# A tenth SBUF home for expert tiles, TensorE's experts written out, down bias behind the transposes, last tile in three pieces, output stores from two queues

## The chip, the cores and the metric

One core of one Trainium2 chip. The metric is the device time of one execution of the program, in microseconds (us).

## The reference

One inference step of a one-layer trunk, over T = 320 tokens (256 of a prompt, 64 of a sample) with 1024 features, in float32:

```python
x += W_out [ GatedDeltaNet heads | MLA heads ]( RMSNorm(x) )
x += MemXAttn( RMSNorm(x), mem )          # 4 heads, 256 memory tokens
x += MoE( RMSNorm(x) )                    # top 4 of 32 experts, softmax router

# MoE, for each expert e and its tokens xb
gu = xb @ w_gu[e] + b_gu[e]               # 1024 -> 2048
gt = min(gu[:, :1024], 7); up = clip(gu[:, 1024:], -7, 7)
act = gt * sigmoid(1.702 * gt) * (up + 1)
y = act @ w_down[e] + b_down[e]           # 1024 -> 1024, then times the gate, summed per token
```

The weights of one expert are 8 MB (w_gu) and 4 MB (w_down); all 32 experts are read.

## The kernel before, in words

**Before the experts** (up to about 360 us) come the input projection, the delta-rule heads, the latent attention, the output projection (its matmuls count the semaphore x2_mm), the attention over the memory and the router. SyncE (SP) issues all weight loads from one queue, each behind `wait_ge` on the semaphores that say that the place in SBUF is free.

**The expert stream.** An expert's weights are TILES = 6 tiles of 2 MB: four of w_gu (GT = 4, each 256 rows of K) and two of w_down (512 rows each). Tile number n (0 to 191) goes to home n % SLOTN of SLOTN = 9 homes of 16 KB a partition (`slot_sb`, L277, `tile_at`, L279): six lie in the tensor `weights`, one each in `stream`, `small_weights` and `more_weights`. Nine tiles are loaded before the experts start (`first_tiles`, L544 to L558), each as soon as its place is free: tiles 2 to 5, then 8, 0, 7, 6, and 1. From then on tile n is issued when TensorE has used tile n - 9 (`refill`, L560: `wait_ge(tile_used)`, then one DMA, in a loop of 18 tiles, which are 3 experts). One DMA is spread over 16 DMA engines, and its semaphore is full when all of them have landed their part.

**One expert on TensorE** (`expert`, L1920): `gate_up` (L1844) multiplies the gathered tokens, 64 of them, with four tiles and lays the scatter of the expert before between them (matmuls with the one-hot rows `slotT`, then DVE's `accumulate`, L2576, adds into x); `gather` (L1832) collects the tokens of the next expert with 60 bf16 matmuls, and `slots_to_rows` makes three transposes; `down` (L1878) waits for the activation, transposes it (four transposes, L1125), waits for ScalarE's copies of them (`copies`, L1099) and multiplies with the two w_down tiles; ScalarE then copies the 64 rows out. The bias of w_down is put into the PSUM bank first by `down_bias` (L1838, two bf16 matmuls, with the row selector `sel` that DVE's `select`, L2482, writes), called in `gate_up` behind the second k. Experts 1 to 30 stand in a hardware loop of ten turns with three experts each (L1926); expert 31 is written behind it (L1929), expert 0 ahead of it. Where the program says `matmul` on float32 the trace shows two weight loads and two matmuls.

**On DVE** a loop over experts (accumulate, `slotT` copy, one-hot slots, activations, `select`, and `rows_in`, L2555, which copies the gathered tokens out) runs beside it. What follows the last expert is a branch for experts with more than 64 tokens, which these inputs do not take (no instruction of it is in the trace).

**The end.** The last scatter gives five halves of x. DVE adds each (L2584), and SP stores it once `acc_done` says so (`store_half`, L576 to L580): six DMAs from SP's queue, the fifth and the sixth both behind the fifth addition.

**Tables.** The router's small tables (`KT`) lie in `stream`, `om` (the memory attention's output) and `wr_sb` (the router's weights) in the first part of it.

Of the kernel before, what the change touches and what calls it, by code (L numbers as in the profile page):

```python
# [15 lines left out]
BF16 = mybir.dt.bfloat16  # L16
# [5 lines left out]
P = 128  # L22
# [66 lines left out]
def trunk_kernel(nc, x_prompt, x_sample, cache_kv_latent, cache_k_rope, state_gdn, state_conv, cache_mem_k,  # L89
# [5 lines left out]
    with ctx:  # L95
# [162 lines left out]
        om = V[:, 4352:5632].rearrange("p (h t) -> p h t", h=H)  # L258
# [17 lines left out]
        GT, TILES, SLOTN, TURN = 4, 6, 9, 3  # L276
        slot_sb = [W[:, 4 * FF * n:4 * FF * (n + 1)] for n in range(6)] + [VK[:, 5888:9984], RH[:, 2816:6912], W2[:, :]]  # L277
# [4 lines left out]

        def fixed(e):

            return [tile_at(TILES * e + t) for t in range(TILES)]

        def turned(i, c):

            return [(ap, name, i * (16 * TURN * TILES // SLOTN) + count)
                    for ap, name, count in (tile_at(TILES * (1 + c) + t) for t in range(TILES))]  # L290

        def extra(j):

            return [(slot_sb[t], f"ld_slot{t}", j * 16 + 16 * ((TILES * E - t + SLOTN - 1) // SLOTN + 1)) for t in range(TILES)]
# [10 lines left out]
        wr_sb = V[:, 5632:5888].rearrange("p (k n) -> p k n", k=KD)  # L305
# [10 lines left out]
        rpos = KT[:, 256:388].rearrange("p (b e) -> p b e", b=TB + 1)  # L316
        xg_pair = PS[4][:, :].rearrange("p (a k t) -> p a k t", a=2, k=4)
        lg = KT[:, 452:560].rearrange("p (b e) -> p b e", b=TB)
        mrep = KT[:, 560:668].rearrange("p (b e) -> p b e", b=TB)
        top8 = KT[:, 668:692].rearrange("p (b e) -> p b e", b=TB)  # L320
        rep8 = KT[:, 692:716].rearrange("p (b e) -> p b e", b=TB)
        S = KT[:, 716:908].bitcast(BF16).rearrange("p (b a s) -> p b a s", b=TB, a=2)
        identb, ustrictb, onesb = (X[:, 2560 + 64 * i:2624 + 64 * i].bitcast(BF16) for i in range(3))
        id3 = X[0:96, 2752:2769].bitcast(BF16)
        cnt, tot, start = KT[0:E, 988:989], KT[0:E, 989:990], KT[0:E, 990:991]
        flags, pos4 = KT[0:E, 992:996], KT[0:E, 996:1000]
        hot = KT[0:E, 1000:1128].rearrange("p (b s) -> p b s", b=XTRA)
        xlist = KT[:, 1128:1200].bitcast(I32)
        ntop = KT[:, 1200:1203]
        gsum = KT[:, 1203:1206]  # L330
# [31 lines left out]
        for b in range(2):  # L362
            for h in range(H):
# [4 lines left out]
                                  [[vm_p[:, i, h * P:(h + 1) * P] for i in range(2)]], om[:, h:h + 1, qs]))  # L368
        qs, ks = slice(2 * P, T), slice(SEQ, NKEY)
        for h in range(0, H, 2):  # L370
# [6 lines left out]
                              [[vm_s[:, i, j * P:(j + 1) * P] for i in range(2)] for j in two], om[:, h:h + 2, qs]))  # L377
# [54 lines left out]


# [4 lines left out]
        def _(sp):  # L438
# [137 lines left out]
            def store_half(b, half):  # L576
                cols = slice(512 * half, 512 * half + 512)
                dst = yp[0][b * P:(b + 1) * P, cols] if b < 2 else ys[0][:, cols]
# [6 lines left out]
            with sp.If(n_extra > 0):  # L585
# [6 lines left out]
                for n in range(2 * TB):  # L592
                    store_half(n // 2, n % 2)
# [2075 lines left out]
```

## Time and profile before

| | us |
|---|---|
| median of 3 runs | 1284.6 (1284.45 to 1285.82) |
| the profiled execution's own time | 1286.58 |
| its span (first to last instruction) | 1284.8 |
| TensorE busy in the span | 1252.6 |
| DVE busy | 436.9 |
| ScalarE busy | 207.1 |

The profiled execution took 1.78 us more than its span, and 1.98 us more than the median. "PE" is TensorE's matmuls, "PEld" its weight loads, "SPq" what SyncE's queue issues, L and a number a line of the kernel. L1122 and L1125 are helpers through which all matmuls and all plain transposes go.

### The profile page before, as it was taken

What the parts mean: (1) busy time and instruction counts of PE and PEld (TensorE: products, weight loads), DVE (VectorE), ACT (ScalarE), POOL (GpSimd) and SP (SyncE); (2) the same over time, 40 slices, a digit from 0 to 9 for tenths busy, and PEclk for the clock granted to TensorE, in tenths of its full rate; (3) what the DMA queues carried; (4) which work ended last, traced back from release to release, by engine and by line L of the source; (5) the groups of instructions that cost most, each with busy time, mean ns of one, the idle gap of its engine ahead of it and who ended that gap; (6) DMA issues with size and microseconds to landing.
All of it is one profiled execution on the core that took longest, in us unless ns stands there. A gap on an engine that the chain in (4) does not pass through costs nothing.

```text
span 1284.8 us, 20003 instructions
## 1 busy us (share of the span) xinstructions
PE 1252.6 (97%) x8107; PEld 569.6 (44%) x8107; DVE 436.9 (34%) x970; ACT 207.1 (16%) x551; POOL 17.2 (1%) x30
## 2 busy tenths in 40 slices
PE   8999999999999999999999999999999999999997
PEld 6677654576543333333333333333333333333332
DVE  4454334535552222223222222332222233222223
ACT  2542433722420000000000000000000000000000
POOL 0000001100000000000000000000000000000000
PEclk8999999999989999999999999999999999999999
DMA  9611010963359999999999999999999999999996
GB/s 313 252 66 67 2 30 17 320 274 132 135 228 429 427 427 428 429 428 428 428 428 428 428 428 430 428 429 428 429 428 429 428 429 428 428 428 429 428 428 265
DMA packets 48768, 439.06 MB, mean 342 GB/s; under 512 B 8677, under 2 KB 11213, under 8 KB 24058
## 3 DMA queue, kind: packets, MB, share of 16 engines
q1 hardware_dynamic: 48492, 438.32, 82.0%
q8 instruction: 28, 0.46, 0.1%
q10 hardware_dynamic: 238, 0.20, 0.1%
q14 instruction: 10, 0.08, 0.0%
HBM read 435.17 MB, written 3.33 MB: 341 GB/s over the span
## 4 chain that ended last, share of the span: by engine, by line
PE 80%; DMA 16%; ACT 2%; DVE 1%; issue 1%; DVEq 0%; SPq 0%; ACTq 0%
PE bank L1122 77%; DMA weights<-in_w_gu 16%; PE bank L1125 2%; ACT scaled L643 1%; DMA x<-in_x_sample 1%; PE bank L1829 0%; ACT stream L643 0%; DVE x L2584 0%; DVE scaled L2446 0%; DVE stats L2343 0%; ACT weights L643 0%; DVE scaled L2029 0%; DVE x L2239 0%; DVEq L2624 0%; DVE small_weights L2424 0%
## 5 line engine op out<-in xcount | busy, mean ns | idle before, releaser
L2584 DVE SCALAR_TENSOR_TENSOR x<-bank,small_weights,x 128x512 f32<-128x512 f32 x160 | 114.0, 747 | 599.4 <-PE bank L1122 599.4
L1122 PE MATMUL bank<-weights,small_weights 128*64 128x512 f32 x1360 | 308.7, 596 | 3.9 <-DMA weights<-in_w_gu 3.2
L1122 PEld LDWEIGHTS bank<-weights,small_weights 128*64 128x64 f32 x1360 | 92.3, 136 | 189.2 <-issue 169.5
L1122 PE MATMUL bank<-weights,scaled 128*64 128x512 f32 x704 | 155.9, 595 | 5.1 <-ACT scaled L643 5.1
L1122 PE MATMUL bank<-small_weights,weights 128*128 128x320 f32 (+4 forms) x400 | 111.2, 426 | 0.0
L643 ACT ACTIVATE scaled<-bank 128x512 f32<-128x512 f32 (+7 forms) x148 | 55.5, 403 | 341.3 <-PE bank L1122 245.2
L1122 PE MATMUL bank<-scaled,small_weights 64*128 64x512 f32 (+1 forms) x320 | 108.0, 641 | 0.7 <-ACT scaled L643 0.7
L643 ACT ACTIVATE scaled<-scaled 128x512 f32<-128x512 f32 x32 | 20.2, 630 | 531.7 <-DVE scaled L1960 531.7
L1122 PEld LDWEIGHTS bank<-weights,scaled 128*64 128x64 f32 x704 | 48.7, 137 | 97.1 <-issue 87.8
L1122 PEld LDWEIGHTS bank<-stream 128*128 128x128 bf16 (+2 forms) x2068 | 73.3, 100 | 28.6 <-issue 28.0
L1122 PEld LDWEIGHTS bank<-small_weights,weights 128*128 128x128 f32 (+2 forms) x400 | 72.6, 192 | 28.2 <-issue 2.2
L1122 PE MATMUL bank<-stream,small_weights 128*64 128x512 f32 (+2 forms) x360 | 82.6, 583 | 1.5 <-DMA stream<-in_w_gu 1.5
L1122 PE MATMUL bank<-stream 128*128 128x64 bf16 (+3 forms) x2068 | 80.0, 203 | 0.4 <-DVE stream L1956 0.4
L1122 PE MATMUL bank<-small_weights 128*64 128x512 f32 (+2 forms) x344 | 75.9, 517 | 0.0
L1122 PEld LDWEIGHTS bank<-scaled,small_weights 64*128 64x128 f32 (+1 forms) x320 | 28.9, 185 | 78.4 <-issue 75.9
L1122 PE MATMUL bank<-weights 64*64 64x64 f32 (+5 forms) x752 | 62.4, 266 | 0.0
L1122 PE MATMUL bank<-small_weights,stream 128*128 128x320 f32 (+4 forms) x212 | 54.4, 410 | 0.5 <-DVE small_weights L2357 0.5
L1122 PEld LDWEIGHTS bank<-weights 64*64 64x64 f32 (+3 forms) x752 | 38.1, 144 | 22.1 <-issue 21.1
L1122 PEld LDWEIGHTS bank<-stream,small_weights 128*64 128x64 f32 (+1 forms) x360 | 25.8, 139 | 49.8 <-issue 43.5
L1122 PEld LDWEIGHTS bank<-small_weights 128*64 128x64 f32 (+2 forms) x344 | 25.9, 132 | 45.6 <-issue 44.4
L1122 PEld LDWEIGHTS bank<-small_weights,stream 128*128 128x128 f32 (+1 forms) x212 | 35.2, 187 | 15.0 <-issue 1.9
L1122 PE MATMUL bank<-more_weights,small_weights 128*64 128x512 f32 x176 | 40.2, 598 | 0.5 <-DMA more_weights<-in_w_gu 0.5
(216 smaller groups left out, 893.1 us busy)
## 6 DMA issues: line engine op xcount, KB each, us to landing
weights<-in_w_gu SPq DMA_DIRECT2D x85, 2048.0 KB, 27.3
weights<-in_w_down SPq DMA_DIRECT2D x44, 2048.0 KB, 28.7
stream<-in_w_gu SPq DMA_DIRECT2D x21, 2048.0 KB, 28.4
more_weights<-in_w_gu SPq DMA_DIRECT2D x11, 2048.0 KB, 28.1
small_weights<-in_w_gu SPq DMA_DIRECT2D x11, 2048.0 KB, 26.6
small_weights<-in_w_down SPq DMA_DIRECT2D x10, 2048.0 KB, 28.5
more_weights<-in_w_down SPq DMA_DIRECT2D x10, 2048.0 KB, 28.8
weights<-in_w_in SPq DMA_DIRECT2D x3, 2048.0 KB, 14.0
```

What stands on the lines that cost most here:

```text
L643: return act.activation(out, in_, func, **kw)
L1122: return pe.matmul(out, lhsT, rhs, start=start, stop=stop)
L1125: return pe.transpose(out, in_, ident[0:in_.shape[0], 0:in_.shape[0]])
L2584: dve.scalar_tensor_tensor(xx, PS[bank][:, :], gcur[:, b:b + 1], xx, ALU.mult, ALU.add)\
```

## The change

- `SLOTN` 9 to 10. The tenth home is VK[:, 7936:12032] in `stream`, and the seventh moves to VK[:, 3840:7936]. To make room `KT` goes from `stream` to `small_weights`, `om` to three other pieces of `stream`, `wr_sb` to `x`.
- The order of the first loads is now tiles 2 to 5, 6, 8, the router's weights, 0, 7, 1, and tile 9 behind the router's last matmul (`lg_mm`). Before, the router's weights went ahead of tile 8, and tile 6 came late. SP's refill loop has 30 tiles (TURN = 5) instead of 18.
- TensorE's loop over experts is gone: experts 1 to 31 are written out one behind the other, with waits on constants.
- `down_bias` moves out of `gate_up` to behind the four transposes in `down`. DVE does `rows_in` first and then waits for the bias matmuls before `select`.
- The last tile (191) is loaded by three DMAs (k rows 0 and 1; 2; 3) with a semaphore each, and TensorE waits for each piece where it needs it.
- The second, fourth and sixth output store are issued by ScalarE, the others by SP.

The diff, cut to what the text speaks of:

```diff
-        KT = KV[:, 2816:4096]
+        KT = R[:, 1956:2816]
-        om = V[:, 4352:5632].rearrange("p (h t) -> p h t", h=H)
+        om = [V[:, 1536:2048].rearrange("p (h t) -> p h t", h=H), V[:, 2048:2560].rearrange("p (h t) -> p h t", h=H),
+              V[:, 3072:3328].rearrange("p (h t) -> p h t", h=H)]
-        GT, TILES, SLOTN, TURN = 4, 6, 9, 3
-        slot_sb = [W[:, 4 * FF * n:4 * FF * (n + 1)] for n in range(6)] + [VK[:, 5888:9984], RH[:, 2816:6912], W2[:, :]]
+        GT, TILES, SLOTN, TURN = 4, 6, 10, 5
+        slot_sb = [W[:, 4 * FF * n:4 * FF * (n + 1)] for n in range(6)] + [VK[:, 3840:7936], RH[:, 2816:6912], W2[:, :], VK[:, 7936:12032]]
+        LAST, LAST_PARTS = tile_at(E * TILES - 1), ((0, 2), (2, 3), (3, 4))
-        wr_sb = V[:, 5632:5888].rearrange("p (k n) -> p k n", k=KD)
+        wr_sb = X[:, 2769:3025].rearrange("p (k n) -> p k n", k=KD)
...
             sp.wait_ge(sem("x2_mm"), KD)
+            first_tiles(TILES, TILES + 1)
+            sp.wait_ge(sem("x2_add"), KD)
+            first_tiles(8, 9)
+            sp.wait_ge(sem("b3_step"), 12)
             load(wr_sb, k_major(w_router[0], 0, KD), "ld_wr")
-            sp.wait_ge(sem("x2_add"), KD)
-            first_tiles(SLOTN - 1, SLOTN)
             sp.wait_ge(*at("qm_mm"))
             first_tiles(0, 1)
             sp.wait_ge(sem("att_s"), ATT["mem"] + UNITS)
-            first_tiles(TILES + 1, SLOTN - 1)
-            sp.wait_ge(sem("att_pv"), ATT["mem"] + 2 * H)
-            first_tiles(TILES, TILES + 1)
+            first_tiles(7, 8)
             sp.wait_ge(sem("x3_mm"), HALVES)
             first_tiles(1, 2)
+            sp.wait_ge(sem("lg_mm"), TB)
+            first_tiles(9, 10)
...
-            for n in range(SLOTN + (E - 2) // TURN * TURN * TILES, E * TILES):
+            for n in range(SLOTN + (E - 2) // TURN * TURN * TILES, E * TILES - 1):
                 sp.wait_ge(sem("tile_used"), n - SLOTN + 1)
...
+            sp.wait_ge(sem("tile_used"), E * TILES - SLOTN)
+            for m, (k0, k1) in enumerate(LAST_PARTS):
+                sp.dma_start(LAST[0][:, FF * k0:FF * k1].rearrange("p (k n) -> p k n", n=FF),
+                             w_down[0, E - 1, 4 * P:8 * P, :].rearrange("(p k) n -> p k n", k=4)[:, k0:k1, :]).then_inc(sem(f"ld_last{m}"), 16)
...
-            for n in range(2 * TB):
+            for n in range(0, 2 * TB, 2):
                 sp.wait_ge(sem("acc_done"), (E - 1) * HALVES + min(n, HALVES - 1) + 2)
-                store_half(n // 2, n % 2)
+                store_half(sp, n // 2, n % 2)
...
+            for n in range(1, 2 * TB, 2):
+                act.wait_ge(sem("acc_done"), (E - 1) * HALVES + min(n, HALVES - 1) + 2)
+                store_half(act, n // 2, n % 2)
...
-                    if between is None and k == 1:
-                        down_bias()
...
+                down_bias()
                 for n in range(2):
                     pe.wait_ge(sem("actT_ev"), it * 2 + 1)
-                    pe.wait_ge(sem(tiles[GT + n][1]), tiles[GT + n][2])
+                    last = tiles[GT + n] is LAST
+                    if not last:
+                        pe.wait_ge(sem(tiles[GT + n][1]), tiles[GT + n][2])
                     for k in range(4):
+                        for m, (k0, k1) in enumerate(LAST_PARTS):
+                            if last and k == k0:
+                                pe.wait_ge(sem(f"ld_last{m}"), 16)
...
-            with pe.Fori(0, (E - 2) // TURN) as i:
-                for c in range(TURN):
-                    expert(i * TURN + (1 + c), turned(i, c))
-            for e in range(1 + (E - 2) // TURN * TURN, E):
+            for e in range(1, E - 1):
                 expert(e, fixed(e))
+            expert(E - 1, fixed(E - 1)[:-1] + [LAST])
...
+                rows_in(it + 1)
+                dve.wait_ge(sem("bias_mm"), it + 1)
                 select(it + 1)
-                rows_in(it + 1)
```

## Rows read from the trace of the kernel before

**Rows 1.** The page: busy time of the engines; GB/s in 40 slices of 32 us.

```profile
PE 1252.6 (97%) x8107; PEld 569.6 (44%) x8107; DVE 436.9 (34%) x970; ACT 207.1 (16%) x551; POOL 17.2 (1%) x30
GB/s 313 252 66 67 2 30 17 320 274 132 135 228 429 427 427 428 429 428 428 428 428 428 428 428 430 428 429 428 429 428 429 428 429 428 428 428 429 428 428 265
```

**Rows 2.** The chain that ended last: start us, length us, what.

```profile
442.54 27.25 PE bank L1122 x172
470.72 27.25 PE bank L1122 x172
498.90 27.25 PE bank L1122 x172
...
1006.14 27.25 PE bank L1122 x172
1034.32 10.98 PE bank L1122 x52
1045.49 39.70 DMA weights<-in_w_gu
...
1221.07 40.31 DMA weights<-in_w_gu
1261.42 5.83 PE bank L1122 x76
```

**Rows 3.** Stretches: busy us (and count) of PE, PEld, DVE, ACT, POOL; clock; DMA share; GB/s.

```profile
364.50:371.40 6.90, 6.29 (x54) 3.66 (x53) 3.96 (x15) 2.14 (x5) 0.00 (x0) 0.85 0.00 0
600.00:684.54 84.54, 83.85 (x539) 31.51 (x537) 24.33 (x45) 5.66 (x12) 0.00 (x0) 1.00 1.01 429
20.00:475.00 455.00, 447.16 (x3016) 263.11 (x3016) 197.14 (x519) 147.75 (x423) 17.04 (x26) 0.99 0.51 199
```

**Rows 4.** SP's queue around the first experts, and TensorE's last router matmul, in time.

```profile
356.82 0.33 SPq L440 DMA_DIRECT2D weights<-in_w_gu  x1
371.49 0.35 SPq L564 DMA_DIRECT2D weights<-in_w_gu  x1
...
360.09 0.43 PE L1122 MATMUL bank<-gain_rows,scaled 128*64 128x32 f32 x4 [0.34 <-ACT scaled L643]
```

**Rows 5.** DMA, issues from 371.4 (tile 9) and 463 (tile 29): median us to landing.

```profile
weights<-in_w_gu SPq DMA_DIRECT2D x1, 2048.0 KB, 7.8
...
463.15 0.33 SPq L564 DMA_DIRECT2D weights<-in_w_down  x1
weights<-in_w_down SPq DMA_DIRECT2D x1, 2048.0 KB, 15.2
```

**Rows 6.** DMA queues, of 20 to 475 us, 382 to 384, and 475 to 1260: packets, MB, share.

```profile
q8 instruction: 25, 0.41, 0.4%
...
q8 instruction: 1, 0.02, 3.1%
...
q1 hardware_dynamic: 23097, 336.36, 100.7%
```

**Rows 7.** The last expert in time, TensorE and SP's queue.

```profile
1222.02 0.41 PE L1122 MATMUL bank<-gain_rows,small_weights 96*64 96x512 bf16 x2
1222.27 3.65 PE L1122 MATMUL bank<-weights,small_weights 128*64 128x512 f32 x16
1225.96 5.22 SPq L572 DMA_DIRECT2D weights<-in_w_down  x2
...
1267.26 0.69 PE L1125 MATMUL bank<-const,scaled 128*128 128x128 f32 x4
1268.18 7.09 PE L1122 MATMUL bank<-weights,scaled 128*64 128x512 f32 x32 [0.23 <-ACT scaled L643]
```

**Rows 8.** The end in time: DVE's last additions, SP's stores, the last two stores' landing.

```profile
1277.20 3.38 DVE L2584 SCALAR_TENSOR_TENSOR x<-bank,small_weights,x 128x512 f32<-128x512 f32 x5 [9.14 <-PE bank L1122]
1280.61 0.51 SPq L580 DMA_DIRECT2D out<-x  x1
1281.16 0.79 SPq L580 DMA_DIRECT2D out<-x  x1
out<-x SPq DMA_DIRECT2D x2, 128.0 KB, 3.0
```

More of the change, by code:

```diff
@@ L367, in trunk_kernel @@
                 mem_units.append(([[(qmT[:, h, qs], km_p[:, h, :])]], NMEM, False,
-                                  [[vm_p[:, i, h * P:(h + 1) * P] for i in range(2)]], om[:, h:h + 1, qs]))
+                                  [[vm_p[:, i, h * P:(h + 1) * P] for i in range(2)]], om[b][:, h:h + 1, :]))
         qs, ks = slice(2 * P, T), slice(SEQ, NKEY)
@@ L376, in trunk_kernel @@
             mem_units.append(([[(qmT[:, j, qs], km_s[:, j, :]) for j in two]], NMEM, False,
-                              [[vm_s[:, i, j * P:(j + 1) * P] for i in range(2)] for j in two], om[:, h:h + 2, qs]))
+                              [[vm_s[:, i, j * P:(j + 1) * P] for i in range(2)] for j in two], om[2][:, h:h + 2, :]))
         CS_AT = 2
@@ L428, in sums_so_far, with store_half @@
             return len(squared)
+        def store_half(queue, b, half):
+            cols = slice(512 * half, 512 * half + 512)
+            dst = yp[0][b * P:(b + 1) * P, cols] if b < 2 else ys[0][:, cols]
+            rows = x3[:, b, cols] if b < 2 else x3s[CH * half:CH * half + CH, :]
+            queue.dma_start(dst, rows).then_inc(sem("st_out"), 16)
         block = ctx.enter_context(nc.Block())
@@ L572, in _ @@
                 sp.dma_start(dst, tile_rows(n // TILES, n % TILES, True)).then_inc(sem(name), 16)
+            sp.wait_ge(sem("tile_used"), E * TILES - SLOTN)
+            for m, (k0, k1) in enumerate(LAST_PARTS):
+                sp.dma_start(LAST[0][:, FF * k0:FF * k1].rearrange("p (k n) -> p k n", n=FF),
+                             w_down[0, E - 1, 4 * P:8 * P, :].rearrange("(p k) n -> p k n", k=4)[:, k0:k1, :]).then_inc(sem(f"ld_last{m}"), 16)
             sp.wait_ge(*at("list_ready"))
             n_extra = sp.value_load(xlist[0:1, 2 * LIST:2 * LIST + 1], min_val=0, max_val=LIST - 1)
-            def store_half(b, half):
-                cols = slice(512 * half, 512 * half + 512)
-                dst = yp[0][b * P:(b + 1) * P, cols] if b < 2 else ys[0][:, cols]
-                rows = x3[:, b, cols] if b < 2 else x3s[CH * half:CH * half + CH, :]
-                sp.dma_start(dst, rows).then_inc(sem("st_out"), 16)
-            for n in range(2 * TB):
+            for n in range(0, 2 * TB, 2):
                 sp.wait_ge(sem("acc_done"), (E - 1) * HALVES + min(n, HALVES - 1) + 2)
-                store_half(n // 2, n % 2)
+                store_half(sp, n // 2, n % 2)
             with sp.If(n_extra > 0):
@@ L592, in _ @@
                 for n in range(2 * TB):
-                    store_half(n // 2, n % 2)
+                    store_half(sp, n // 2, n % 2)
                 sp.wait_ge(sem("st_out"), 16 * (4 * TB))
@@ L1663, in mem_out @@
                 for h in range(H):
-                    m = mm(PS[6 + half][0:rows, :], om[:, h, b * P:b * P + rows], wmo_sb[:, h, 512 * half:512 * half + 512],
+                    m = mm(PS[6 + half][0:rows, :], om[b][:, h, :], wmo_sb[:, h, 512 * half:512 * half + 512],
                            h == 0, h == H - 1)
@@ L1674, in mem_out_pair @@
                     for side in range(2):
-                        m = mm(PS[4][half(side), :], om[:, h, 2 * P:2 * P + DEC], wmo_sb[:, h, 512 * side:512 * side + 512],
+                        m = mm(PS[4][half(side), :], om[2][:, h, :], wmo_sb[:, h, 512 * side:512 * side + 512],
                                h == 0, h == H - 1)
```

41 lines of the change are left out of this document (18 added, 23 removed).

## The prediction

> **What bounds the kernel now.** I read the page first. TensorE is busy for 97% of the span, which reads like a kernel bound by TensorE, but the line of GB/s stands at 427 to 430 from the thirteenth slice to the last but one, whatever else happens [rows 1]. So I took the chain that ended last, in order of time. Up to 1034 us it goes from expert to expert on TensorE, 28.18 us apart (442.54, 470.72, 498.90, 27.25 of it matmuls and gather, the rest the wait for the transposed activation). From 1045 us it hangs on the landing of tiles: each link is 40 us of DMA, and the last of them ends at 1261.38, with 23.4 us behind it [rows 2].
>
> The two periods belong together. Tile 29 is issued at 463.15 and lands 15.2 us later, at 478.35; tile 189, the last of w_gu, lands at 1221.07 + 40.31 = 1261.38 [rows 2, 5]. That is 160 tiles in 783.03 us, 4.894 us each, 29.4 us for an expert's six. The stream is slower than TensorE's 28.18 us an expert and never idle once the refills run. TensorE merely eats a lead of nine tiles until 1034 us and then waits. **The end is therefore the time at which the stream becomes continuous, plus 4.894 us for each tile still to come, plus whatever else the DMA engines must do, plus a tail.** What TensorE saves per expert moves only the point at which it starts to wait.
>
> The stream becomes continuous at 371.49 us, when tile 9 is issued. Tile 1 was issued at 356.82, and from 364.5 to 371.4 us the DMA moved nothing (share 0.00) [rows 3, 4].
>
> **The tenth home.** Its tile 9 no longer waits for a used tile but for the router's last matmul, which starts at 360.09 and takes 0.43 us, so the issue comes at about 360.6 [rows 4]. Tile 1 is then on its way until about 364.5; tile 9 follows without a gap and lands near 364.5 + 4.9 = 369.4, inside the idle stretch. Tile 10 is issued at 371.49 in its place, and every later tile takes the place that its predecessor had. I count the whole tile: **-4.9 us**. Bounds: -4.9 if nothing of it collides, and 0 if the first uses on TensorE slip by a tile's length; I see no reason for such a slip, since the new order only moves tile 6 and the router's weights among loads that land twenty or more us ahead of their first use. The stream keeps ten tiles ahead instead of nine, so no refill is late.
>
> **TensorE's experts written out.** For TensorE itself I charge nothing and credit nothing: periods within and across the turns of the loop are the same 28.18 us (the back branch of a three-expert turn is in one of the three periods shown), and the first turn, whose code was new, ran at that pace too [rows 2]. But instructions come by DMA. The instruction queue q8 shows 25 packets of 16 KB from 20 to 475 us, and not one from 475 to 1260 us, where only q1 has packets [rows 6]: the loop's code stays in place once it has been read. Written out, the code of 27 more experts (31 minus the four that were written down before) must be fetched beside the stream. In 84.54 us, three experts, 537 weight loads were counted, 179 an expert and as many matmuls, so 358 instructions; from 20 to 475 us 3016 + 3016 of them went with 25 packets, 241 to a packet [rows 3, 6]. 27 x 358 / 241 = **40 more packets**, all inside the saturated stretch.
>
> What does one cost? In a stretch of 2 us one such packet had 3.1% of 16 engines' time, 0.99 us on one engine [rows 6]. If the 40 are spread evenly, that is 40 x 0.99 / 16 = 2.5 us of the stream. A second price comes from landings: tile 9 landed at 371.49 + 7.8 = 379.3, tile 29 at 478.35, 20 tiles in 99.05 us where 20 x 4.894 makes 97.9. The stream lost 1.16 us in exactly the stretch in which the code of the loop came in (six 16 KB packets from 381 us on and two half ones), and nothing in the 160 tiles behind it. A tile is there when the last of 16 engines is there, so this 1.16 us is what one packet costs the engine that ends last. Eight packets have hit eight engines at most once; 48 make three rounds of 16, so the engines that end last get two or three more hits: 2.3 to 3.5 us. I take 2.7 rounds at 1.16, **+3.1 us**, near the upper end because a late engine never catches up in a saturated stream. Ends kept for the range: 0 (packets slip into gaps) and 10 (see the rivals).
>
> The Trainium skill (Runtime: NRT & Kernel Launch, section Instruction fetch mechanics) says that crossing a 16 KB block of instructions costs "one DMA tail-bump, mostly hidden", and recommends full unrolling. That agrees with TensorE's unchanged pace above; of the stream it would make the charge nothing, and the sum 3.1 us lower.
>
> **Down bias behind the transposes.** Its two matmuls delay the next ones by 0.25 us (1222.02 to 1222.27) in a place where TensorE waits for the next tile anyway, so removing them there gives nothing at the end. In their new place they stand in the last chain: transposes from 1267.26 for 0.69 us, then a wait for ScalarE's copy until 1268.18 [rows 7]. They fit into that gap of 0.23 us and the modelled tail of the transposes; bounds 0 and +0.25, taken 0. DVE's new wait before `select` has the next `accumulate` queued behind it, whose scatter comes 12 us later, and TensorE asks for `sel` 7 us later; the activation is ahead of it. If that cover went, it would cost the 0.25 us once an expert, and still nothing in a stream-bound stretch.
>
> **The last tile in pieces.** SP issues tile 190 at 1225.96 and tile 191 at the end of the 5.22 us, 1230.85; with 40.3 us to landing it is there at 1271.15. TensorE starts the down matmuls at 1268.18 and takes 7.09 us for both tiles, so it comes to tile 191 at 1271.72, 0.57 us after the landing [rows 7]. There is no wait to remove: 0. Two more issues in SP's queue, 0.33 us each, come 30 us ahead of need.
>
> **Stores from two queues.** The fifth store is issued at 1280.61, the sixth at 1281.16, held up by 0.51 us of issue, and takes 0.79 us itself [rows 8]. Both wait for the same addition. With ScalarE issuing the sixth, idle by then, it goes out at 1280.6 too. Its landing at 1281.16 + 3.1 = 1284.3 (3.0 is the median of both) could come at 1283.5. Bounds -0.8 and 0 (both share the engines); taken **-0.6 us**, near the 0.55 between the two issues.
>
> **Sum**: -4.9 + 3.1 + 0 + 0 + 0 - 0.6 = -2.4 us. On the profiled execution that is a span of 1282.4 and a time of 1284.2 for 1286.58; on the median, 1.98 us under the profiled time, **1282.2 us**, 0.19% faster. Some 0.2% (2.57 us) is what a measurement of this kernel can tell from no change, so this forecast sits on the line between faster and the same; its own range is 1280.9 to 1283.6.
>
> **Rivals.**
> *Pages are free.* The 40 packets fall where an engine would have lost nothing. For it: bandwidth in the slices of the first turn is 427 and later 428, hardly a difference [rows 1]. Against it: the 1.16 us lost between tile 9 and tile 29. -4.9 - 0.6 = -5.5: 1279.1 us.
> *The fetch queue uses few engines.* The late landings show only that the last engine was late once in eight packets. Suppose that q8 goes round six engines rather than 16. By 1260 us it has brought 6 + 40 = 46 packets since the stream became continuous; the worst engine carries 8, seven more than before, 7 x 1.16 = 8.1 us. The result is -4.9 + 8.1 - 0.6 = +2.6 us: 1287.2, slower. It decides from six engines downwards; at eight it would be five more, 5.8 us, and +0.3. For it: nothing in these rows names an engine. Against it: six packets in the first turn cost the last landing no more than one did, so at least about six engines were used.
> *The tenth home gives nothing*, since tile 9 is late or the first use slips: +3.1 - 0.6 = +2.5 us, 1287.1. It needs the idle stretch [rows 3] to vanish; no step of the change shows how.
>
> **From here to the numbers.** The forecast has 0.70, and as it lies on the line, 0.28 of it counts as faster, 0.42 as the same. Free pages 0.13 (faster), few engines 0.10 (slower), no gain from the home 0.07 (just the same). Faster 0.41, same 0.49, slower 0.10. The range goes from the free pages, 1279.1, to 1284.8, which takes in a charge of up to 5 us and a tail that gives nothing; above it lie few engines and most of the last case.
>
> **What would show it.** Right: q8 with some 40 packets between 475 and 1260 us; tile 9 issued near 360.6 and no idle stretch of 7 us behind it; TensorE at 28 us or a little less per expert until it starts to wait; the last w_gu tile landing near 1259.6 instead of 1261.4, and the mean distance of landings 4.91 instead of 4.894; two stores issued at the same time at the end. Wrong: distances of 4.894 (pages free), landings spread ever wider and the last tile behind 1261 (few engines), an issue of tile 10 well behind 371.5 (the home gives nothing), a wait of TensorE at an expert's start (fetch stalls TensorE itself).

## The result, and the profile after

The changed kernel takes 1288.84 us (median of 10 runs, 1286.78 to 1289.2). The kernel before, run beside it, takes 1285.87 us (10 runs, 1284.45 to 1287.17; the three shown ahead had 1284.6). The ratio is 1.002 with a 95% interval of 1.0012 to 1.0028: **2.6 us slower, between 1.5 and 3.6** (the medians lie 3.0 us apart). The prediction was 1282.2, with a range up to 1284.8, so the change went the other way than forecast, and the time lies above the range.

The profiled execution of the changed kernel took 1286.78 us, its span 1285.0. It is the lowest of the ten, most likely because its stream began early: the first refill of a used home was issued at 368.82 us, where the kernel before issued it at 371.49 [rows 4]. Over all profiles of this study that issue came anywhere from 368.8 to 372.8 us. So every comparison of streams below counts from that issue, and not from the start of the span.

The page of the changed kernel, its first part, the line of GB/s and the row of q8, and last the row of q8 on the page of the kernel before:

```profile
PE 1253.0 (98%) x8107; PEld 568.5 (44%) x8107; DVE 443.3 (35%) x970; ACT 207.2 (16%) x551; POOL 17.2 (1%) x30
...
GB/s 313 252 66 68 1 30 33 318 260 159 108 330 428 428 428 426 428 427 427 428 426 429 426 428 427 427 428 427 428 426 429 426 428 427 426 428 427 427 428 209
...
q8 instruction: 66, 1.08, 0.3%
...
q8 instruction: 28, 0.46, 0.1%
```

Each engine runs as many instructions as before. The twelfth slice (353 to 385 us) moves 330 GB/s where 228 stood before. That is 3.3 MB more: 2.1 MB of it the tenth tile, the rest about what the first refill's earlier issue brings. From the thirteenth slice on it is 426 to 429 where 427 to 430 stood [rows 1], a difference of the last digit, too small to read a cause from. The instruction queue q8 brings 66 packets of code (16 KB each) in the whole span, 28 before.

The stream's start in SP's queue, and its first ten tiles' last landing (issue at 358.33, mean us to landing):

```profile
354.70 0.33 SPq L443 DMA_DIRECT2D weights<-in_w_gu  x1
358.33 0.33 SPq L443 DMA_DIRECT2D stream<-in_w_gu  x1
368.82 0.35 SPq L569 DMA_DIRECT2D weights<-in_w_down  x1
...
stream<-in_w_gu SPq DMA_DIRECT2D x1, 2048.0 KB, 9.6
```

Tile 9 goes out 10.5 us ahead of the first refill, and is there at 358.33 + 9.6 = 367.9. Of the idle stretch of 6.9 us [rows 3] only the 0.9 us from this landing to the first refill are left, much as forecast.

The chain that ended last, in order of time:

```profile
466.83 27.29 PE bank L1128 x172
494.83 27.29 PE bank L1128 x172
...
914.73 7.34 PE bank L1128 x34
922.22 42.80 DMA stream<-in_w_gu
...
1216.48 45.02 DMA stream<-in_w_gu
1261.54 5.83 PE bank L1128 x76
```

TensorE now needs 28.00 us an expert (466.83 to 494.83) where it needed 28.18, and for all that it begins to wait for tiles at 922 us instead of 1045, although it starts with one tile more in hand. The last link of DMA ends at 1216.48 + 45.02 = 1261.50, against 1261.38 before [rows 2].

The links of DMA in this chain, each from the issue of a tile to its landing, are 42.8 to 45.7 us long where 39.7 to 40.3 stood. That is not the loss. Once TensorE waits for tiles, a refill is issued as many landings ahead as there are homes, and a tenth home adds one landing, 4.9 us. The last links of the runs below agree: 35.31 us with eight homes (b_8x4), 40.31 and 40.30 with nine (b_out with 39 packets of code and m_late with 5), 45.02 with ten. The loss is seen in the pace of the landings: tile 29 lands at 470.68 and tile 189 at 1261.50, **4.943 us a tile where 4.894 stood, 7.8 us in 160 tiles.** The forecast was 4.91.

The DMA queues of the saturated stretch, 475 to 1260 us, and a stretch of three experts in it (600 to 684 us, columns as in rows 3):

```profile
q1 hardware_dynamic: 23062, 334.80, 100.3%
q8 instruction: 38, 0.62, 0.3%
```

```profile
600.00:683.97 83.97, 83.97 (x538) 31.60 (x537) 24.90 (x45) 5.66 (x12) 0.00 (x0) 1.00 1.01 428
```

There are 38 packets of code where none came before [rows 6]; 40 were forecast. In the three experts shown TensorE is busy all the time at the full clock (1.00), so the fetch doesn't stall it there. What it delays is seen only when a tile's landing is taken apart into its 16 arrivals, one from each DMA engine. The trace gives their times and not the engines' names. In each row comes first the time at which the tile is complete, then the 16 arrivals in order, in us after the first of them:

```
before landed  379.33  0.0 0.1 0.2 0.2 0.2 0.4 0.4 0.4 0.4 0.5 0.5 0.5 0.6 0.6 0.7 1.0
before landed  497.91  0.0 0.1 0.2 0.3 0.4 0.4 0.6 0.8 1.2 1.3 1.4 1.5 1.6 1.8 1.8 2.0
before landed 1261.38  0.0 0.1 0.2 0.3 0.4 0.4 0.6 0.9 1.2 1.4 1.4 1.5 1.7 1.8 1.9 2.0
after  landed  376.54  0.0 0.0 0.3 0.3 0.3 0.4 0.4 0.4 0.4 0.5 0.5 0.6 0.6 0.7 0.9 0.9
after  landed  500.41  0.0 0.2 0.3 0.4 0.4 0.6 0.8 1.0 1.0 1.9 1.9 1.9 2.0 2.0 2.0 2.4
after  landed  747.82  0.0 0.0 0.1 0.1 0.4 0.6 0.8 0.8 2.8 3.1 3.2 3.3 3.7 4.7 4.7 4.9
after  landed  999.29  0.0 0.1 0.1 0.2 0.5 0.7 0.9 0.9 4.3 6.2 6.3 6.3 6.3 6.4 6.5 6.8
after  landed 1261.50  0.0 0.2 0.2 0.2 0.6 0.8 0.9 1.0 7.5 7.8 8.0 8.5 9.4 9.4 9.4 9.7
```

Here is the whole result. Before, while the code of the loop's first turn is read, the last arrival goes from 1.0 to 2.0 us behind the first, and from 498 to 1261 us the picture moves by 0.1 us at most. After, eight arrivals stay within 1.0 us of each other, and the other eight fall back step by step to 7.5 to 9.7 us. The first arrival keeps the old pace: from tile 29 to tile 189 it takes 4.894 us a tile in both kernels. A tile is usable when its last sixteenth is there, so TensorE and the refills see only the slow eight: 9.7 us behind where 2.0 stood is 7.7 us lost, and against it stands the 4.9 us of the tenth home.

The last expert, TensorE in time, and SP's queue ahead of it:

```profile
1267.38 0.70 PE L1131 MATMUL bank<-const,scaled 128*128 128x128 f32 x4
1268.01 0.41 PE L1128 MATMUL bank<-gain_rows,small_weights 96*64 96x512 bf16 x2
1268.31 7.09 PE L1128 MATMUL bank<-weights,scaled 128*64 128x512 f32 x32
...
1225.77 11.84 SPq L580 DMA_DIRECT2D weights<-in_w_down  x3
```

The down bias stands behind the transposes and the down matmuls start 0.93 us behind them; before, 0.92 us [rows 7]. The 7.09 us are the same too: no piece of the last tile was waited for, before or now. The row of SP holds the three issues of these pieces; they took 0.34, 1.10 and 10.32 us (forecast 0.33 each), ahead of need, so this cost nothing. From the landing at 1261.50 to the first of the last additions (1277.32) it is 15.82 us, and it was 15.82 before (1261.38 to 1277.20) [rows 2, 8]. The end, in time, and then the issues of 1280.6 to 1280.8 us with their us to landing:

```profile
1277.32 3.38 DVE L2591 SCALAR_TENSOR_TENSOR x<-bank,small_weights,x 128x512 f32<-128x512 f32 x5 [8.39 <-PE bank L1128]
1278.10 3.14 SPq L435 DMA_DIRECT2D out<-x  x3
...
out<-x SPq DMA_DIRECT2D x1, 128.0 KB, 2.6
out<-x ACTq DMA_DIRECT2D x1, 128.0 KB, 3.7
```

The two last stores leave together right behind the last addition, which the sixth followed 0.5 us later before [rows 8], but the one from ScalarE takes 3.7 us where some 3.1 did.

### The profile page after: what moved, and what is told of

Its sections match the earlier page's. It is cut to its first block, busy times and chain, and to the rows that moved or that the text cites. A ratio compares the mean times of both kernels' runs of the same rounds, so it can differ in the third digit from the quotient of the medians.

```text
span 1285.0 us, 19747 instructions
## 1 busy us (share of the span) xinstructions
PE 1253.0 (98%) x8107; PEld 568.5 (44%) x8107; DVE 443.3 (35%) x970; ACT 207.2 (16%) x551; POOL 17.2 (1%) x30
## 4 chain that ended last, share of the span: by engine, by line
PE 75%; DMA 21%; DVE 1%; ACT 1%; issue 1%; ACTq 0%; DVEq 0%; SPq 0%
PE bank L1128 72%; DMA weights<-in_w_gu 11%; DMA stream<-in_w_gu 7%; DMA small_weights<-in_w_gu 4%; PE bank L1131 3%; DMA stream<-in_kv_a_norm 0%; PE bank L1835 0%; ACT stream L646 0%; DVE x L2591 0%; ACT scaled L646 0%; ACTq L652 0%; DVE scaled L2453 0%; DVE stats L2350 0%; ACT weights L646 0%; DVE small_weights L1963 0%
## 5 line engine op out<-in xcount | busy, mean ns | idle before, releaser
L1128 PE MATMUL bank<-weights,small_weights 128*64 128x512 f32 x1216 | 276.9, 597 | 7.0 <-DMA weights<-in_w_gu 6.4
L1128 PEld LDWEIGHTS bank<-weights,small_weights 128*64 128x64 f32 x1216 | 81.6, 136 | 185.3 <-issue 158.2
L1128 PE MATMUL bank<-weights,scaled 128*64 128x512 f32 x640 | 142.1, 595 | 0.6 <-DMA weights<-in_w_down 0.6
L1128 PE MATMUL bank<-small_weights,stream 128*128 128x64 bf16 (+6 forms) x2192 | 129.6, 220 | 0.8 <-DVE small_weights L2364 0.5
L1128 PEld LDWEIGHTS bank<-small_weights,stream 128*128 128x128 bf16 (+2 forms) x2192 | 104.8, 107 | 41.4 <-issue 27.9
L1128 PE MATMUL bank<-stream,small_weights 128*64 128x512 f32 (+2 forms) x440 | 101.0, 586 | 3.3 <-DMA stream<-in_w_gu 3.3
L1128 PE MATMUL bank<-small_weights 128*64 128x512 f32 (+2 forms) x376 | 83.2, 524 | 1.1 <-DMA small_weights<-in_w_gu 1.1
L1128 PE MATMUL bank<-more_weights,small_weights 128*64 128x512 f32 x208 | 47.3, 596 | 1.3 <-DMA more_weights<-in_w_gu 1.3
L1128 PE MATMUL bank<-stream,scaled 128*64 128x512 f32 x192 | 43.5, 595 | 0.0
L1968 DVE TENSOR_SCALAR scaled<-bank 128x512 f32<-128x512 f32 x32 | 22.1, 692 | 32.8 <-PE bank L1128 32.8
```

The source lines that it names most:

```text
L1128: return pe.matmul(out, lhsT, rhs, start=start, stop=stop)
L1968: return dve.tensor_scalar(out, a, s1, s2, op0, op1)
```

## The experiments

My theory after the result: code packets go to eight of the 16 engines, each costs its engine 1.5 us or so, and 38 of them cost the stream more than the tenth home gives. Rivals: the tenth home gives nothing (first use slipped, or tiles land in a worse order), or the moved bias, the pieces or the stores cost something. What is measured from each run's one trace is the time from the issue of the first refill to the landing of tile 189, the last of w_gu; "over" is that time minus 4.894 us for each of the 181 tiles (nine homes), 180 tiles (ten homes) or 182 tiles (eight homes) that are issued from there on up to tile 189. Times are medians; the ratio is to the kernel before on the same chip.

### Written out alone, and rolled up again alone

**b_out**: the kernel before, with experts 1 to 31 written out and nothing else.

```diff
-            with pe.Fori(0, (E - 2) // TURN) as i:
-                for c in range(TURN):
-                    expert(i * TURN + (1 + c), turned(i, c))
-            for e in range(1 + (E - 2) // TURN * TURN, E):
+            for e in range(1, E):
                 expert(e, fixed(e))
```

> The kernel before (nine homes) with experts 1 to 31 written out on TensorE, nothing else. Fetch theory with eight engines: 38 packets more, 4.75 rounds of eight at 1.5 us, +7 to +7.7 us, ratio 1.0055 to 1.006. My prediction's price (16 engines, 1.16 us): +3.1 us, 1.0024. Rival that the tenth home is at fault: 1.000.

Measured: 1293.52 us, ratio 1.0048 [1.0032, 1.0065], a little under the forecast, which the interval still holds. Its first refill in SP's queue, its chain's last link of DMA and its packets of 475 to 1260 us:

```profile
370.80 0.35 SPq L564 DMA_DIRECT2D weights<-in_w_gu  x1
```

```profile
1228.17 40.31 DMA weights<-in_w_gu
1268.53 5.83 PE bank L1122 x76
```

```profile
q8 instruction: 39, 0.64, 0.3%
```

From 370.80 to 1268.48 it is 897.68 us, against 889.89 before (371.49 to 1261.38): 7.8 us for 39 packets, with TensorE's work unchanged. The 16 arrivals of tile 189 fall apart as in the changed kernel: eight within 1.2 us, the other eight 7.6 to 9.8 us behind the first. So written-out code is the loss, and **a packet costs the stream 0.20 us**. It also gives the tenth home's worth: the changed kernel has 38 packets, one fewer, and needs 1261.50 - 368.82 = 892.68 us, 5.0 less than this one. That is the one tile of 4.9 us in full.

**a_loop**: the changed kernel with experts 1 to 30 in a loop again, five to a turn, since ten homes repeat after five experts.

```diff
+        def turned(i, c):
...
-            for e in range(1, E - 1):
+            with pe.Fori(0, 6) as i:
+                for c in range(TURN):
+                    expert(i * TURN + (1 + c), turned(i, c))
+            for e in range(1 + 6 * TURN, E - 1):
                 expert(e, fixed(e))
```

> The changed kernel with TensorE's experts 1 to 30 in a loop again (five experts a turn, six turns), all else as changed. Fetch theory (each 16 KB packet of TensorE's code holds one of eight DMA engines up by 1.5 us, and the tile is there when the worst of them is): some 3 packets more than in the kernel before and none after the first turn, so the tenth home's 4.9 us show, less up to 1.5 us: ratio to the kernel before 0.996 to 0.998, the landings 4.894 us apart after the first turn. Rival (the tenth home or the new order of the first loads costs time, the code costs 3 us at most): ratio 1.000 or above.

Measured: 1290.33 us, ratio 1.0031 [1.002, 1.0041]. This missed: the loop didn't give the loss back. Its packets of 475 to 1260 us, and its chain around the second turn:

```profile
q8 instruction: 48, 0.79, 0.4%
```

```profile
496.93 27.29 PE bank L1133 x172
524.92 7.32 PE bank L1133 x34
534.20 20.16 PE bank L1133 x138
...
1220.37 44.66 DMA stream<-in_w_gu
```

There are more packets than in the written-out kernel, not fewer. Five experts are some 5 x 370 = 1850 instructions (179 weight loads and as many matmuls an expert were counted, a dozen others is an estimate), and this body is read anew in every turn, some eight packets a turn. At a turn's start TensorE even waits: 524.92 + 7.32 = 532.24, and the next row begins at 534.20, 2 us with nothing. A packet of code begins at 531.45 and takes 1.07 us, so the wait is most likely one for code. The stream takes 1265.03 - 370.84 = 894.19 us, over by 13.3: 9.2 more than the kernel before, 0.19 us for each of 48 packets. So the theory's price stood, and what fell was my belief that any loop keeps its code.

**a_half** (the changed kernel, three turns of five in a loop, the other experts written out) was meant to halve the packets:

```diff
+        def turned(i, c):
...
-            for e in range(1, E - 1):
+            with pe.Fori(0, 3) as i:
+                for c in range(TURN):
+                    expert(i * TURN + (1 + c), turned(i, c))
+            for e in range(1 + 3 * TURN, E - 1):
                 expert(e, fixed(e))
```

> The changed kernel with 15 experts in a loop (three turns of five) and 16 written out. Fetch theory: about 22 packets fewer than written out in full, less than three rounds of eight, so 3 to 4.5 us less than the changed kernel and about the time of the kernel before (ratio 0.999 to 1.000). If being written out cost by its mere form (TensorE slower, or one event), not by the packet: equal to one of the two ends, 0.997 or 1.002.

Measured: 1289.8 us, ratio 1.0025 [1.0013, 1.0037], over by 11.8 with 42 packets (below). This missed too: as a loop of five is read anew each time, it halved nothing and told nothing apart.

**b_turn6** (the kernel before, TURN = 6 for 3): the same nine homes and a loop of six experts, some 2200 instructions.

```diff
-        GT, TILES, SLOTN, TURN = 4, 6, 9, 3
+        GT, TILES, SLOTN, TURN = 4, 6, 9, 6
```

> The kernel before with six experts a turn instead of three (five turns), nine homes. The loop's code is then about 2200 instructions instead of 1100. If it stays in place as that of three does: about 4 packets more, +0 to +1.5 us, ratio 1.000 to 1.001. If code of more than some 2048 instructions is read anew each turn (the Trainium skill, Runtime: NRT & Kernel Launch, Instruction fetch mechanics, gives TensorE 2048): packets all the way as in the written-out form, +7 us, ratio 1.0055.

Measured: 1293.94 us, ratio 1.0058 [1.0041, 1.0074]: 1268.54 - 369.46 = 899.08 us, over by 13.3. Here TensorE has the same wait, 1.9 us at the turn of 560 us and 2.1 at that of 731. The rows of packets from 475 to 1260 us, of a_half and then of b_turn6:

```profile
q8 instruction: 42, 0.69, 0.4%
```

```profile
q8 instruction: 48, 0.79, 0.4%
```

### Where a loop's code stays, and how the loss grows

**b_half**: the kernel before, five turns of its three experts, then experts 16 to 31 written out.

```diff
-            with pe.Fori(0, (E - 2) // TURN) as i:
+            with pe.Fori(0, 5) as i:
                 for c in range(TURN):
                     expert(i * TURN + (1 + c), turned(i, c))
-            for e in range(1 + (E - 2) // TURN * TURN, E):
+            for e in range(1 + 5 * TURN, E):
```

> The kernel before (nine homes, three experts a turn) with five turns and experts 16 to 31 written out. Does the loss grow with the packets, or is it there at once? Fetch theory: about 22 packets more, in the second half of the stream alone, 30 in all, four hits an engine instead of one or two: the last w_gu tile lands 4 to 5 us later after the first refill's issue than in the kernel before, ratio 1.003 to 1.004. If it is there at once: 1.0055 as in b_out, or 1.000.

Measured: 1290.31 us, ratio 1.0035 [1.0022, 1.0049]; 21 packets, 1263.83 - 369.24 = 894.59 us, over by 8.8 where the kernel before is over by 4.1. That is 4.7 us for 21 packets, 0.22 each. Its rows, packets and then the chain's last DMA landing:

```profile
q8 instruction: 21, 0.34, 0.2%
```

```profile
1263.87 5.83 PE bank L1122 x76
```

**b_8x4**: the kernel before with eight homes and four experts a turn, some 1480 instructions.

```diff
-        GT, TILES, SLOTN, TURN = 4, 6, 9, 3
+        GT, TILES, SLOTN, TURN = 4, 6, 8, 4
...
-            first_tiles(SLOTN - 1, SLOTN)
...
-            first_tiles(TILES + 1, SLOTN - 1)
+            first_tiles(TILES + 1, SLOTN)
```

> Eight homes and four experts a turn (seven turns, experts 29 to 31 written out), else the kernel before. It asks how long a loop TensorE's code memory keeps: three experts (about 1110 instructions) stay, five (about 1850) are read anew each turn. If the border is 2048 less a read-ahead of less than 570, four (about 1480) stay: some 12 packets in the stream. If it is below 1480: 50 or more. The time is about 5 us worse for the missing home, plus 1 or 9 us for the packets.

Measured, one execution only: 1292.61 us, with these packets from 475 to 1260 us:

```profile
q8 instruction: 4, 0.07, 0.0%
```

The first of the four comes at 500 us, in the first turn, and the others from 1206 us on, where experts 29 to 31 are written out. So a loop of about 1110 instructions (the kernel before) and one of about 1480 stay, one of about 1850 and one of about 2200 are read anew each turn; where between 1480 and 1850 the border lies wasn't tried.

All kernels side by side. The last column is how far the last of the 16 arrivals of tile 189 is behind the first:

| kernel | homes | q8 packets 475 to 1260 us | first refill to tile 189, us | over, us | last arrival behind first, us |
|---|---|---|---|---|---|
| before | 9 | 0 | 889.89 | 4.1 | 2.0 |
| b_bias | 9 | 0 | 890.03 | 4.2 | 2.0 |
| b_stores | 9 | 0 | 890.11 | 4.3 | 2.0 |
| b_8x4 | 8 | 4 | 896.36 | 5.7 | 3.4 |
| b_half | 9 | 21 | 894.59 | 8.8 | 6.5 |
| b_out | 9 | 39 | 897.68 | 11.9 | 9.8 |
| b_turn6 | 9 | 48 | 899.08 | 13.3 | 11.3 |
| after | 10 | 38 | 892.68 | 11.8 | 9.7 |
| a_half | 10 | 42 | 892.74 | 11.8 | 9.7 |
| a_loop | 10 | 48 | 894.19 | 13.3 | 11.3 |
| m_late | 10, then 9 | 5 | 886.55 | 5.6 | 3.2 |
| m_best | 10, then 9 | 5 | 887.49 | 6.6 | 4.3 |
| m_one | 10, then 9 | 1 | 887.23 | 6.3 | 1.9 |
| m_home | 10, then 9 | 2 | 888.09 | 7.2 | 2.0 |

The two right columns belong together. In all rows but the last two, "over" is the last column plus 2.0 to 2.4 us, whatever the homes, the form of the code or the small edits (the last two have a hole in their stream, see below). So what code adds to the time is the distance of the slowest engine from the fastest. In the six runs with 21 packets or more this is 0.18 to 0.22 us a packet above the kernel before. In each of these six the arrivals of tile 189 fall into halves: the first eight within 0.8 to 1.7 us, the ninth 4.4 us or more behind the first. If eight engines take turns, a packet's price is 1.5 to 1.8 us for each hit. With few packets it goes by steps: the same 5 packets put the slowest engine of m_late 1.2 us further back than in the kernel before, and that of m_best 2.3.

### The small edits, each alone

**b_bias**: the kernel before with the down bias behind the transposes and DVE's new order.

```diff
-                    if between is None and k == 1:
-                        down_bias()
...
+                down_bias()
                 for n in range(2):
...
+                rows_in(it + 1)
+                dve.wait_ge(sem("bias_mm"), it + 1)
                 select(it + 1)
-                rows_in(it + 1)
```

> The kernel before with the down bias behind the transposes and DVE's new order alone. Stream theory: TensorE's expert takes 28.0 instead of 28.18 us and begins to wait earlier or later, the end does not move, ratio 1.000. Rival (it stands in the last chain and costs): up to +0.25 us, too little for the ratio, but the time from the last w_gu landing to the down matmuls would be 7.0 instead of 6.76 us.

Measured: 1286.18 us, ratio 1.0001 [0.9991, 1.001]. Two experts of its chain, and its last expert on TensorE:

```profile
440.66 27.29 PE bank L1122 x172
468.65 27.29 PE bank L1122 x172
```

```profile
1267.18 0.41 PE L1122 MATMUL bank<-gain_rows,small_weights 96*64 96x512 bf16 x2
```

27.99 us an expert instead of 28.18: the two matmuls now lie in the wait for ScalarE's copies. TensorE is faster by this, and it is worth nothing at the end, since the stream sets the end.

**b_stores**: the kernel before with every second output store from ScalarE's queue.

```diff
-            for n in range(2 * TB):
+            for n in range(0, 2 * TB, 2):
                 sp.wait_ge(sem("acc_done"), (E - 1) * HALVES + min(n, HALVES - 1) + 2)
...
+            for n in range(1, 2 * TB, 2):
+                act.wait_ge(sem("acc_done"), (E - 1) * HALVES + min(n, HALVES - 1) + 2)
+                store_half(act, n // 2, n % 2)
```

> The kernel before with the output stores from SP and ScalarE in turn, alone. My prediction: -0.6 us, the sixth store issued 0.5 us earlier and landed 0.6 earlier, DVE's last addition to the end 3.6 us instead of 4.2. As the changed kernel's trace now suggests: issued earlier, landed at the same distance from the last addition, 0.

Measured: 1286.45 us, ratio 1.0002 [0.9993, 1.0012]. Its last two issues, with their us to landing:

```profile
out<-x SPq DMA_DIRECT2D x1, 128.0 KB, 2.5
out<-x ACTq DMA_DIRECT2D x1, 128.0 KB, 4.0
```

From the end of the last addition to the end of the span it has 4.51 us, the kernel before 4.18. Over all profiles this tail is 4.2 to 4.4 us with stores from SP alone and 4.2 to 4.5 from two queues, so a loss isn't shown either. The sixth store leaves 0.5 us earlier and lands no earlier. The Trainium skill (DMA: Bandwidth & Descriptors, section Issuing engines are not separate DMA queues) says that a second issuing engine only saves the sequencer's time to issue, because the transfers run on the same 16 engines; the two rows agree.

The pieces of the last tile weren't run alone. That they do nothing rests on the unchanged 15.82 us above.

### Ten homes with a loop that stays

Ten homes repeat after five experts, which is too long a loop; nine repeat after three. The tenth home is needed only while tile 9 fills the idle stretch. So: start with ten homes, go on with nine, and loop over three experts.

**m_one**: ten homes for tiles 0 to 9 only, nine from tile 10, experts 2 to 31 in ten turns of three; the last tile whole, the other edits kept. **m_home** is the same with the down bias and the stores as in the kernel before.

```diff
-        GT, TILES, SLOTN, TURN = 4, 6, 10, 5
+        GT, TILES, SLOTN, TURN = 4, 6, 10, 3
...
-            return slot_sb[n % SLOTN], f"ld_slot{n % SLOTN}", 16 * (n // SLOTN + 1)
+            h, loads = (n, 1) if n < SLOTN else ((n - SLOTN) % 9, 2 + (n - SLOTN) // 9)
+            return slot_sb[h], f"ld_slot{h}", 16 * loads
...
+            def refill_once(n):
+                sp.wait_ge(sem("tile_used"), n - 9 if n < 19 else n - 8)
...
-            for e in range(1, E - 1):
-                expert(e, fixed(e))
-            expert(E - 1, fixed(E - 1)[:-1] + [LAST])
+            expert(1, fixed(1))
+            with pe.Fori(0, (E - 2) // TURN) as i:
+                for c in range(TURN):
+                    expert(i * TURN + (2 + c), turned(i, c))
```

> The tenth home holds tile 9 alone and is then left; tiles from 10 on go round nine homes, so that TensorE's code is as short as before: expert 0 and 1 written out, experts 2 to 31 in ten turns of three. Last tile whole; down bias and stores as changed. Fetch theory: as many packets as in the kernel before (8), so the tenth home's tile shows in full: the last w_gu tile lands 885.0 us after the first refill's issue instead of 889.9, -4.9 us, ratio 0.9955 to 0.9970. Rival (ten homes matter later in the stream, or the changes of layout cost): nearer to 1.000 than 0.998.

> The same with the down bias back in gate_up and all six stores from SP: the tenth home and its order of loads alone. Fetch theory: the same time as m_one within the interval, ratio 0.9955 to 0.9970.

Measured: m_one 1284.49 us, ratio 0.999 [0.9981, 0.9999]; m_home 1284.09 us, ratio 0.9984 [0.9975, 0.9993]. Less than expected, and the two intervals overlap, so the bias and the stores make no difference that shows here either. m_home's SP queue, and its stretch of 418 to 424 us (columns as in rows 3):

```profile
408.13 0.33 SPq L579 DMA_DIRECT2D more_weights<-in_w_gu  x1
419.74 3.71 SPq L574 DMA_DIRECT2D weights<-in_w_gu  x2
```

```profile
418.00:424.00 6.00, 6.00 (x32) 2.10 (x30) 0.00 (x0) 0.60 (x1) 0.00 (x0) 1.00 0.69 235
```

Giving up a home means that one refill waits for two more used tiles instead of one. Here that is tile 19: SP issues nothing from 408.13 to 419.74 us, the tiles on their way run out, and the DMA engines stand at 0.69 for 6 us: 1.9 us of the stream lost at once. The arrivals show more. From the tile complete at 421.04 us to the one complete at 427.32 the last arrival goes from 2.2 to 0.6 us behind the first: in the hole the late engines catch up, while the early ones lose 3.0 us.

**m_best** goes over to nine homes at tile 20 (the refill that waits for two is tile 29), with experts 1 to 3 and 31 written out and nine turns of three between them; stores from two queues, bias moved.

```diff
+            h, loads = (n % SLOTN, n // SLOTN + 1) if n < 2 * SLOTN else ((n - 2 * SLOTN) % 9, 3 + (n - 2 * SLOTN) // 9)
...
-            for e in range(1, E - 1):
+            for e in range(1, 1 + OUT):
                 expert(e, fixed(e))
-            expert(E - 1, fixed(E - 1)[:-1] + [LAST])
+            with pe.Fori(0, 9) as i:
+                for c in range(TURN):
+                    expert(i * TURN + (1 + OUT + c), turned(i, c))
+            expert(E - 1, fixed(E - 1))
```

> Ten homes as in the changed kernel for the first 20 tiles, then nine in rotation, which lets TensorE's loop have three experts a turn again (experts 4 to 30 in nine turns; 1, 2, 3 and 31 written out); last tile whole; the rest as changed. Fetch theory: 12 or 13 packets in the saturated stretch against 8 in the kernel before and 46 in the changed one, so at most two hits on an engine: -4.9 + 1.5 = -3.4 us or better against the kernel before, ratio 0.996 to 0.998. Rival (the tenth home itself costs): 1.000 or above.

Measured: 1282.31 us, ratio 0.9971 [0.996, 0.9982], as expected. At the step SP issues nothing from 452.26 to 461.73 us, and the DMA engines stand at 1.01 from 450 to 470 us: no hole.

**m_late** goes over at tile 30 (the refill that waits for two is tile 39), later in the stream, with experts 0 to 4 written out and 5 to 31 in nine turns of three; the stores come from SP alone.

```diff
+            h, loads = (n % SLOTN, n // SLOTN + 1) if n < 30 else ((n - 30) % 9, 4 + (n - 30) // 9)
...
-            for e in range(1, E - 1):
+            for e in range(1, 5):
                 expert(e, fixed(e))
-            expert(E - 1, fixed(E - 1)[:-1] + [LAST])
+            with pe.Fori(0, 9) as i:
+                for c in range(TURN):
+                    expert(i * TURN + (5 + c), turned(i, c))
```

> Ten homes in rotation for tiles 0 to 29 and nine from tile 30 on, when SP's queue is deeper than in m_one and m_home, where the change at tile 10 left the DMA idle for about 2 us near 420. Experts 0 to 4 written out, 5 to 31 in nine turns of three, stores from SP alone. Fetch theory: no idle stretch at 420 or later; about 12 packets of code, two or three hits on the worst engine; last w_gu tile 885.5 to 888 us after the first refill's issue, ratio 0.996 to 0.9978. If the hole in m_home was not the reason for its smaller gain: 0.9984 as there.

Measured: 1281.3 us (6 runs, 1280.88 to 1282.8) against 1286.14, ratio 0.9967 [0.9955, 0.9979]. Its first refill, its chain's last link of DMA, and its packets:

```profile
369.81 4.06 SPq L579 DMA_DIRECT2D weights<-in_w_down  x2
```

```profile
1216.05 40.30 DMA stream<-in_w_gu
```

```profile
q8 instruction: 5, 0.08, 0.0%
```

Five packets instead of 38, and no hole: at the step SP issues nothing from 499.92 to 507.40 us, and the DMA engines stand at 1.01 from 500 to 520 us. It needs 1256.35 - 369.81 = 886.5 us, 3.3 less than the kernel before, which is 4.9 for the tenth tile less 1.6. Of these, 1.2 are the last arrival, 3.2 us behind the first where 2.0 stood; what the other 0.4 are stays open. It beats the kernel before by 0.33%, and its median is 7.5 us under that of the changed kernel, which ran at another time.

## Why the prediction was wrong

**What bounds the kernel: right.** The end was the start of the continuous stream plus 4.894 us a tile plus what else the DMA engines do plus a tail, in every kernel here. The tail from tile 189 to the first of the last additions was 15.8 to 15.9 us in all of them. TensorE's 0.18 us an expert bought nothing.

**The tenth home, -4.9: right.** Tile 9 was issued at 358.33, 2.3 us before the forecast 360.6, as the router's last matmul started at 357.98 in this execution and not at 360.09. With packets as good as equal (39 and 38) the stream is 5.0 us shorter (b_out against the changed kernel).

**The count of packets, 40: right,** 38. **Their price, +3.1: this step failed, and it alone turned the sign.** The price was a number of rounds times the cost of a hit, 2.7 x 1.16, and both factors were too small. "If the 40 are spread evenly" was false: I spread them over 16 engines. The arrivals show eight engines and 38 / 8 = 4.8 rounds, and the runs show 1.5 to 1.8 us for each hit. The price is 7.8 us. I had the rival with the right mechanism, a queue that uses few engines, and worked it out for eight: "five more, 5.8 us, and +0.3". With 0.10 it got far too little, and 1.16 us a hit was too low even there. The 1.16 came from the landing of the last engine alone, over tiles 9 to 29. At tile 9 the last arrival was 1.0 us behind the first already, at tile 29 it was 2.0. An engine that was 0.5 us behind and is hit once for 1.5 us gives that 2.0 too, so the last arrival moves by less than a hit costs (an estimate, from these rows and b_out). Nor could six packets say how many engines the queue uses, or what a second hit on one costs: eight of the 16 arrivals are 1.2 to 2.0 us late at 498 us, which fits eight engines and rules out no larger number.

The Trainium skill's sentence that I weighed there (Runtime: NRT & Kernel Launch, section Instruction fetch mechanics: crossing a block is "mostly hidden", full unrolling is preferred) holds for TensorE, whose pace b_out leaves unchanged. Of the stream it would make the charge 0 us, and b_out shows 7.8.

**Down bias, 0: right** (b_bias 1.0001). **Last tile in pieces, 0: right** as far as the same 15.82 us shows; that the issues take 0.33 us each was wrong, the last took 10.32. **Stores, -0.6: wrong, and small.** It was about 0 (b_stores 1.0002): the issue was earlier, the landing not. The bound "0 (both share the engines)" was the answer.

The sum by measured terms is -5.0 + 7.8 + 0 + 0 + 0 = +2.8 us. The first two come from three traces, by way of b_out, and add up to the difference of the two kernels' streams by construction; the independent number is the ratio of ten runs each, +2.6 (1.5 to 3.6).

## What to carry to other kernels

In a stretch where DMA sets the time, a kernel's own code is data in the same stream: here 0.2 us for each 16 KB packet, paid by half of the engines. A loop whose body stays in place costs nothing there, and one that is a little too long costs more than no loop at all (1.4 to 1.5 us in the stream here), so look at the instruction queue's packets in the steady state before choosing either. Where a tile waits for all 16 engines, read the arrivals of each one, at an early and a late tile: a mean bandwidth that looks the same hides engines that fall behind. The time from a refill's issue to its landing doesn't tell of a delay either, as it grows with each buffer. And in a stretch that DMA sets, a buffer more is worth just the transfer that it puts into an idle stretch; it can be given up afterwards, when the queue is deep enough to bridge the step.

## What the runs showed of the hardware that was not expected

- Code packets delay eight of the 16 DMA engines. At 1261.5 us these are 7.5 to 9.7 us behind the first, the other seven within 1.0. In b_out it is 7.6 to 9.8 and 1.2.
- A hit costs its engine 1.5 to 1.8 us of the stream, though a packet itself is on its engine for only 0.99 us (3.1% of 16 engines in 2 us [rows 6]). What the rest is, and why there are eight engines, stays open.
- A late engine doesn't catch up while the stream is saturated: the 16 arrivals of the kernel before lie within 0.1 us as they did at 498 us, 763 us later. It does in a hole: in m_home the last arrival went from 2.2 to 0.6 us behind the first.
- Loops of about 1110 and 1480 instructions on TensorE are read once; loops of about 1850 and 2200 are read again every turn, and there TensorE itself stood idle for 1.9 to 2.1 us at a turn's start.
- Three DMAs issued by SP one behind the other into a full stream took 0.34, 1.10 and 10.32 us to issue; the tiles issued one at a time just before took 0.33 to 0.36.
